# POOL's order of the operand sums in a Strassen-Winograd block product: S2 from S3, and S1 after the low parts of S2

## The reference

```python
hm = rmsnorm(x, mlp_norm_g[l]) @ w1[l]
x = x + jnp.square(jax.nn.relu(hm)) @ w2[l]
```

## Time and profile before

| | |
|---|---|
| median of three runs | 2830.46 us (2829.51 to 2834.68) |
| the profiled execution's own time | 2831.85 us |
| its span in the trace | 2830.3 us |
| PE busy | 2812.9 us, 99% of the span |
| DVE busy | 1763.4 us, 62% |
| ACT busy | 1466.8 us, 52% |
| POOL busy | 933.0 us, 33% |
| chain of work that ended last | PE 96% |
| granted TensorE clock | 1.0 |

### The profile page before, as it was taken

The page is one execution under the profiler, slowest core; times in us unless marked ns, Lnnn a source line. Parts: engine busy times, 40 slices in busy tenths (PEclk is TensorE's granted clock), DMA queues, the critical chain, the costliest instruction groups (busy, mean ns, idle before and its releaser), DMA issues.

```text
span 2830.3 us, 44516 instructions
## 1 busy us (share of the span) xinstructions
PE 2812.9 (99%) x15148; PEld 2342.1 (83%) x15148; DVE 1763.4 (62%) x2969; ACT 1466.8 (52%) x3006; POOL 933.0 (33%) x1214
## 2 busy tenths in 40 slices
PE   8999999999999999999999999999999999999998
PEld 8888888888888888888888888888888888888887
DVE  6376765666576755556768675466557675545665
ACT  6554454555455444554645544455545544455553
POOL 5264553444135400242316320044322550023440
PEclk9999999999999999999999999999999999999999
DMA  6732575544542222354454222254454223234442
GB/s 216 249 105 68 175 264 183 190 149 134 135 165 83 76 90 90 112 172 144 146 148 144 68 83 90 90 187 149 131 145 164 83 72 93 90 100 146 149 149 82
DMA packets 178823, 375.50 MB, mean 133 GB/s; under 512 B 13808, under 2 KB 13952, under 8 KB 178592
## 3 DMA queue, kind: packets, MB, share of 16 engines
q1 hardware_dynamic: 155216, 300.45, 34.5%
q0 software_dynamic: 20704, 67.33, 7.2%
q10 hardware_dynamic: 2672, 4.76, 0.5%
HBM read 332.60 MB, written 29.39 MB: 128 GB/s over the span
## 4 chain that ended last, share of the span: by engine, by line
PE 96%; DMA 1%; issue 1%; DVE 1%; ACT 1%; POOL 0%; DVEq 0%; ACTq 0%; POOLq 0%
PE bank L1954 48%; PE work L1954 22%; PE bank L2320 14%; PE work L2320 2%; PE work L1968 1%; PE bank L2358 1%; PE work L2069 1%; DMA vo_dram<-folded 1%; PE bank L1968 1%; PE work L2107 1%; PE work L2129 1%; PE work L2016 1%; PE work L2218 1%; PE work L2222 1%; PE work L2217 1%
## 5 line engine op out<-in xcount | busy, mean ns | idle before, releaser
L875 ACT ACTIVATE w_hi<-raw 128x512 fp32r<-128x512 f32 x1120 | 700.9, 629 | 1031.6 <-PE bank L1954 534.8
L1392 DVE TENSOR_TENSOR w_lo<-raw,w_hi 128x512 fp32r<-128x512 f32 x708 | 510.8, 726 | 840.3 <-ACT w_hi L875 838.9
L1390 DVE SCALAR_TENSOR_TENSOR w_lo<-raw,w_hi 128x512 fp32r<-128x512 f32 x412 | 365.4, 906 | 81.2 <-ACT w_hi L875 80.2
L1954 PE MATMUL bank<-act_hi,w_hi 128*128 128x512 f32 x848 | 333.4, 393 | 0.0
L1954 PE MATMUL bank<-act_lo,w_hi 128*128 128x512 f32 x848 | 330.2, 389 | 0.0
L1954 PE MATMUL bank<-act_hi,w_lo 128*128 128x512 f32 x848 | 330.2, 389 | 0.0
L726 POOL TENSOR_TENSOR hr<-qk 128x256 f32<-128x256 f32 x48 | 35.4, 737 | 770.8 <-ACT qk L1265 770.8
L1954 PE MATMUL bank<-w_hi,act_hi 128*128 128x512 f32 x640 | 255.2, 399 | 0.0
L1954 PE MATMUL bank<-w_lo,act_hi 128*128 128x512 f32 x640 | 249.6, 390 | 0.0
L1954 PE MATMUL bank<-w_hi,act_lo 128*128 128x512 f32 x640 | 249.5, 390 | 0.0
L2320 PE MATMUL bank<-w_hi,h_hi 128*128 128x512 f32 x576 | 224.2, 389 | 0.1
(11 more groups left out here) (391 smaller groups left out, 6073.1 us busy)
## 6 DMA issues: line engine op xcount, KB each, us to landing
raw<-in_w_dram SPq DMA_DIRECT2D x232, 512.0 KB, 3.8
raw<-in_w_in_dram SPq DMA_DIRECT2D x112, 512.0 KB, 3.6
raw<-sums_dram SPq DMA_DIRECT2D x96, 512.0 KB, 3.8
raw<-in_w_out_dram SPq DMA_DIRECT2D x32, 512.0 KB, 4.1
raw<-kq_dram SPq DMA_DIRECT2D x32, 512.0 KB, 3.7
raw<-vo_dram SPq DMA_DIRECT2D x32, 512.0 KB, 3.8
xres<-in_x_dram POOLq DMA_DIRECT2D x16, 512.0 KB, 6.3
early_rows<-in_w_dram POOLq DMA_DIRECT2D x6, 1024.0 KB, 8.4
```

Source lines behind the costliest of these rows:

```text
L875: nc.scalar.activation(w_hi[:, slot, :], raw[:, pair_slot, slot % 2, :], ACT.Copy).then_inc(slab_hi, 1)
L1390: ins = stt(out=w_lo[:, slot, :], in0=src, scalar=1.0, in1=hi, op0=ALU.mult, op1=ALU.subtract)
L1392: ins = tt(w_lo[:, slot, :], src, hi, ALU.subtract)
L1954: ins = mm(dst, left, right, start=(kt == 0 and j == 0), stop=(kt == KT - 1 and j == 2))
```

## The change

S2 is now made from A22 and S3, since A22 - (A11 - A21) = A21 + A22 - A11. It is one operation, which reads `diff` and writes over A11. S1 is no longer needed for S2 and moves behind the low parts of P6. The low parts of P5 now wait on POOL itself for S1.

```diff
                     for kt in range(HALF):
                         pool.wait_ge(hidden_ready, per_pass(g, KT, hb, HALF + kt + 1))
                         pool.wait_ge(diff_ready, per_pass(g, HALF, hb, kt + 1))
-                        nc.gpsimd.tensor_tensor(quarter(0, 1, kt), quarter(0, 1, kt), quarter(1, 1, kt),
-                                                ALU.add).then_inc(s1_ready, 1)
-                        pool.wait_ge(s1_ready, per_pass(g, HALF, hb, kt + 1))
-                        nc.gpsimd.tensor_tensor(quarter(0, 0, kt), quarter(0, 1, kt), quarter(0, 0, kt),
+                        nc.gpsimd.tensor_tensor(quarter(0, 0, kt), quarter(1, 1, kt), diff[:, kt, :],
                                                 ALU.subtract).then_inc(s2_ready, 1)
                     for kt in range(HALF):
                         operand_low(Q_P6, hb, kt, quarter(0, 0, kt))
                     for kt in range(HALF):
+                        nc.gpsimd.tensor_tensor(quarter(0, 1, kt), quarter(0, 1, kt), quarter(1, 1, kt),
+                                                ALU.add).then_inc(s1_ready, 1)
+                    for kt in range(HALF):
+                        pool.wait_ge(s1_ready, per_pass(g, HALF, hb, kt + 1))
                         operand_low(Q_P5, hb, kt, quarter(0, 1, kt))
```

## The result

The changed kernel takes 2838.79 us (median of six runs, 2834.95 to 2845.27), against 2830.53 us for the kernel before (six runs, 2829.51 to 2834.68). The ratio estimated from all twelve runs is 1.0031, with a 95% interval of 1.0021 to 1.0042. By the medians alone the kernel is slower by 8.3 us, or 0.29%. The profiled execution took 2837.18 us and has a span of 2835.5 us, 5.2 us more than before.

The account below looks back on a forecast made before the run. PE, 99% busy, bounds the kernel; lost DVE margin makes it wait. Losses of 1.7, 1.14, 3.7 and 0.45 us make 7.0 us, on the 2830.46 us median 2837.5 us (+0.25%); range 2830.0 to 2845.0.

Parts of the forecast that it names:

- The wait for S2 does not bind: At the start of P6's products, P6's operand comes 2.5 us earlier, which nothing on PE asks for; gain nothing.
- DVE loses more turns to POOL, and PE waits at 0.13 us: In the seven products, POOL and two-SBUF-input DVE operations exclude each other; each lost turn costs DVE 0.57 us of margin.
- Two turns, 1.14 us at slab 12: POOL's later sums of S1 take two more turns from DVE, 2 x 0.57 = 1.14 us; chance 0.42.
- Carried to slab 16 and beyond.: DVE has no slack from slab 10 on, so the 1.14 us delay at slab 12 stays in later slabs.
- split by passes: PE's loss per pass: 0.42 us in the first four, 1.14 in the fifth, 0.92 in the next four, 0.15 in the last three.
- Which slab binds: Slab 16, margin 0.85 us in the first pass, decides; while it stays above 0.7 us, PE loses nothing.
- The stretches: Sign: the seven half-size products of line 2320 take 38.4 to 39.7 us instead of 38.24; staying at 38.24 means forecast wrong.
- margin of slab 16: Sign: time from the slab's low part ending on DVE to its first PE matmul falls from 0.85 to 0.13 us.
- another cause: Sign: if PE's waits name POOL's `h_lo`, the loss does not come from the forecast's mechanism; no size given.
- Three turns: Rival: POOL wins near-ties with DVE, which loses 1.71 us; PE loses 13.8 us, 2844.3 us; chance 0.22 for three or more.
- S1 comes late for ACT: Rival: POOL slips 4 us, ACT stands at 521.01 without S1; each further us costs 12 us in all; chance 0.02.
- one turn or none: Rivals at DVE's slabs: one turn costs 2.0 us, 2832.5 us, chance 0.20; none leaves margins, 2830.5 us, chance 0.14.

## Why the prediction was right, point by point

- **Forecast.** 2837.5 us and +0.25% were forecast, and 2838.8 us came, +0.31% by the ratio and +0.29% by the medians. The sum gave 7.0 us. The profiled execution lost 5.85 us in the products, and the median run 8.3 us.
- **The wait for S2 does not bind.** Right. The last low part of P6 was ready earlier, and the run with S1 back beside S2 shows no gain from the new S2.
- **DVE loses more turns to POOL, and PE waits at 0.13 us.** Right. The runs with less work for DVE, with the sums of S1 cut and with four adds early or late speak against every rival named: take the slack's user away, or POOL's turns, and the loss is gone. The place was only partly right. The prediction put the extra turns at slab 10 and behind. In the first pass the low parts of slabs 8 and 9 lost them, which took 0.67 and 0.68 us before. After, and then slab 9 before (slab 8 is at 515.02 in the earlier trace rows):

```profile
514.25 1.26 DVE L1391 SCALAR_TENSOR_TENSOR w_lo<-raw,w_hi 128x512 fp32r<-128x512 f32 x1
...
516.10 1.25 DVE L1391 SCALAR_TENSOR_TENSOR w_lo<-raw,w_hi 128x512 fp32r<-128x512 f32 x1
```

```profile
516.28 0.68 DVE L1390 SCALAR_TENSOR_TENSOR w_lo<-raw,w_hi 128x512 fp32r<-128x512 f32 x1
```

DVE's second low part of P2 (0.41 us at 520.18 in the earlier trace rows) was to run long in the first pass and stayed at 0.41 us. In the fifth pass it was the first one that ran long.
- **Two turns, 1.14 us at slab 12.** Mis-sized where PE lost time. Slab 12 went from 1.80 to 0.83 us in the first pass, 0.97 us, which is about two turns, and from 1.70 to 1.38 us in the fourth and the seventh, which is less than one. In the fifth it went from 1.76 to 0.18 us, 1.58 us, about three. The third comes because the delayed slab 12 meets the first low part of P5. The prediction took DVE's path behind 521.4 as unchanged, and that step failed.
- **"Carried to slab 16 and beyond."** Wrong in the passes that lost nothing. In the first pass slab 16 had a margin of 1.88 us, more than the 0.85 before, as the last section shows. So the split by passes failed: 0.42 each in the first four was 0, 0.92 each in the next four was 1.25, 0, 1.25 and 1.82, and 0.15 each in the last three was 0.26, 0 and 0. The fifth's 1.14 was 1.31. The sum came out near because errors of both signs met, and that is luck.
- **Which slab binds.** I took 16, and it was 13. In the fifth pass slab 13 has 0.13 us and slab 16 has 0.22.
- **Signs named beforehand.** The stretches were to be 38.4 to 39.7 us. Seven stayed at 38.24, the sign that was named for a wrong forecast, and five took 38.5 to 40.1. The margin of slab 16 was to fall to 0.13 us; it was 0.22 in the fifth pass and grew to 1.88 in the first. PE's waits do not name POOL, which would have meant another cause. POOL's timeline in the first pass:

```profile
510.91 4.05 POOL L716 TENSOR_TENSOR h_lo<-qk,h_hi 128x256 fp32r<-128x256 f32 x4
514.93 4.18 POOL L737 TENSOR_TENSOR qk<-qk 128x256 f32<-128x256 f32 x4
520.98 1.21 POOL L716 TENSOR_TENSOR h_lo<-qk,h_hi 128x256 fp32r<-128x256 f32 x1 [1.87 <-ACT h_hi L1279]
```

The low parts of P6 end at 514.96 and S1 at 519.11, each about 1 us sooner than said, and the idle time is 1.87 us where about 1 was said. Of the 1 us, 0.57 is that the pass itself starts at 506.10 and not at 506.67.

- **Rivals.** Three turns is what four passes of the loop show for slab 12. That S1 comes late for ACT is out, by the run with S1 ahead of the low parts. Of the other eight passes seven cost nothing and one 0.26 us, as with one turn or none. In the seven the reason is one that the prediction did not have: DVE won its time back behind slab 12.

Which passes lose can be read from one operation, POOL's second low part of P5. In the seven passes of the profiled execution that lose nothing, DVE passed it over, as the last section shows, and it took 2.50 to 2.98 us. In the five that lose it took 0.74 to 0.78 us, and either slab 12 (passes 5, 6, 8 and 9) or slab 13 (the tenth) lost a turn to a low part of P5. The tenth pass, POOL and DVE:

```profile
2555.59 0.78 POOL L716 TENSOR_TENSOR h_lo<-qk,h_hi 128x256 fp32r<-128x256 f32 x1 [0.21 <-ACT h_hi L1279]
```

```profile
2555.69 1.23 DVE L1391 SCALAR_TENSOR_TENSOR w_lo<-raw,w_hi 128x512 fp32r<-128x512 f32 x1
```

The run with S1 ahead has such a long operation in two passes, and these lose nothing. The run with the tiny add has it in none, and all twelve lose. What stays open is why DVE passes POOL over in one pass and not in another. The spread of the six runs (2834.95 to 2845.27 us) suggests that it differs between executions too, which no trace here shows. No run beats the kernel before beyond its interval. The products of that kernel hold only 0.55 us of waits, so there was little to win in them.

## What to carry to other kernels

An engine that is two thirds busy on average can be without slack for 20 us of each stage, and there a neighbour's order is part of its path. Before work is moved on one engine, look at which instruction of another gets longer beside it, and at the margin with which its results arrive, slab by slab and not as a mean. Keep shared turns where the other engine waits anyway, as the sums between ACT's squares did.

## What the runs showed of the hardware that was not expected

An operation of POOL that is waiting can be passed over by several of DVE in a row. First pass of the changed kernel, POOL and then DVE:

```profile
522.34 2.98 POOL L716 TENSOR_TENSOR h_lo<-qk,h_hi 128x256 fp32r<-128x256 f32 x1 [0.15 <-ACT h_hi L1279]
```

```profile
522.17 0.41 DVE L1805 SCALAR_TENSOR_TENSOR h_lo<-qk,h_hi 128x256 fp32r<-128x256 f32 x1
522.50 0.68 DVE L1391 SCALAR_TENSOR_TENSOR w_lo<-raw,w_hi 128x512 fp32r<-128x512 f32 x1
523.11 0.41 DVE L1805 SCALAR_TENSOR_TENSOR h_lo<-qk,h_hi 128x256 fp32r<-128x256 f32 x1
523.44 1.28 DVE L1391 SCALAR_TENSOR_TENSOR w_lo<-raw,w_hi 128x512 fp32r<-128x512 f32 x2
```

POOL's operation started at 522.34 and took 2.98 us instead of 0.74. Four of DVE's that started after it ran at full speed. DVE so won back more than it had lost, and from slab 14 on that pass had margins above 0.85 us. It is no single case: seven of the twelve passes of the changed kernel have such an operation of POOL. Elsewhere in these rows the two mostly alternate. The Trainium skill, page "SBUF — State Buffer", section "SBUF: two separate sides", says that whichever starts first gets the pair. These rows go against that, as the first pass of the earlier trace rows does, if starting is what the profile shows as a start. The other statement of that page of the Trainium skill, an exclusive lock for the whole instruction, agrees with the 128 x 8 operation, which took 0.70 us and ended 0.03 us after POOL's.
